# Two stacked transformer blocks on one core: the expert rows are scatter-added to the residual rows instead of being kept in slots and gathered at the end

## The chip, the core and the metric

One core of one Trainium2 chip runs the whole program. The metric is the device time of one execution in microseconds (us); lower is better. The engines are named as in the profile: PE (TensorE; PEld is its weight load), DVE (VectorE), ACT (ScalarE), POOL (GpSimd) and SP (SyncE, which issues most DMAs).

## The reference, cut to what matters

1024 tokens of width 1024 go through a first block of two layers and a second block with a gated mixer and a mixture of experts. The change touches the experts and the final norm:

```python
def _hier_moe(h, ...):            # h: 1024 tokens x 1024
    # softmax over 4 groups, the best group; softmax over its 8 experts, the best TOP_K = 2
    weights = g_p * e_p            # one weight for each (token, choice)
    # the 2048 (token, choice) pairs are sorted by expert and padded to blocks of 128
    yb = (silu(xb @ w_gate[e]) * (xb @ w_up[e])) @ w_down[e]   # hidden width 512
    y = zeros.at[tok_buf].add(yb * w_buf)
# around it:
x = x + gate2 * y
out = x * rsqrt(mean(x * x) + 1e-6) * final_norm_g
```

Counted from the reference on its own inputs, the 2048 pairs spread over the 32 experts with 26 to 129 pairs each (17 experts have 64 or more, one has more than 128).

## The kernel before, in words

The program is a row of stages with a barrier of all engines between them (`Env.run`). The last three matter here.

`stage_mix` writes the residual rows (`x3_rows`, a DRAM tensor of 1024 x 1024) and the normed rows (`n3_rows`). On the side SP stores zeros into a part of `y_slots`, six DMAs of 1280 KB (L2550).

`stage_experts` first routes (DVE, with a few small matmuls on PE): each of the 2048 pairs gets a slot, that is a block of 128 rows and a place in it. Block b < 32 belongs to expert b and is filled from its first partition on; block 32 takes what the fullest expert has over 128. There are `LOOPED` = 33 blocks; code for more stands behind an `If` that is not taken with these inputs. For each block b:

- POOL gathers 128 normed rows by index into `xg` (L3109);
- PE transposes them (L3002), ACT modulates and splits them in a high and a low part (L3167, L3146), DVE makes the low part (L3303);
- PE multiplies with the gate and the up weights, three matmuls (high-high, low-high, high-low) for each of 8 chunks, 24 each (L3007 to L3009);
- ACT applies silu (L3174), DVE multiplies by the up product (`hid`, L3353), PE transposes (L3023), ACT and DVE split again (L3185, L3307), and PE multiplies with the down weights, 24 more matmuls. The down product of block b-1 is made in step b, behind the up product of block b;
- DVE multiplies the result by `gate` into `yb` (`results`, L3314), and SP stores 512 KB of it to block b-1 of `y_slots` (L2926, for the last block L2946).

The weights come in six pieces of 1 MB for each expert: g0, g1, u0, u1, d0, d1. SP loads each to a landing tile as soon as DVE has set it free (L2900), ACT casts it to the high part (`hi`, L3142) when PE has done with the former contents, and DVE subtracts for the low part (`lo`, L3216). PE, ACT and SP run blocks 4 to 29 in a hardware loop; so does DVE. The order of the work on each engine is the order in which the code is written:

```python
def step(b, s):                      # DVE, before
    lo_x(b + 1); lo("g0", b + 1); lo("g1", b + 1)
    # waits for up_full, act_set
    hid = act_ * up_b
    lo("u0", b + 1); results(b - 1); lo("u1", b + 1)
    lo("d0", b); lo("d1", b); lo_h(b)
```

During the last block SP loads the eight tiles of residual rows (`cx`, L2910) and the final gain ahead (L2913).

`stage_combine` gathers, for each of 8 tiles of 128 tokens, the two weighted expert rows of each token from `y_slots` into `cy` (16 indirect DMAs of 512 KB on POOL, L3409). DVE adds the left half with two weighted adds (L3460, L3462), PE the right half in PSUM with diagonal matrices (L3418 to L3428), ACT takes the sums of squares (L3439, L3441) and the root (L3445), DVE scales (L3467, L3468), and SP stores (L3402).

## Time and profile before

| what | value |
|---|---|
| median of 3 runs | 2980.92 us (2980.89 to 2983.64) |
| the profiled execution: its own time | 2982.22 us |
| the profiled execution: its span | 2980.5 us |
| mean granted TensorE clock | 0.984 |
| busy share: PE, PEld, DVE, ACT, POOL | 95%, 72%, 58%, 42%, 15% |
| HBM read, written | 389.78 MB, 61.94 MB |
| experts: first matmul of block 0 to the end of the last | 2327.5 to 2932.3 us |
| last stage: first POOL gather to the end of the span | 2939.55 to 2980.5 us |

The page gives the shares of the whole span. What a change in one stage is worth is read from that stage alone: which wait ends last there, and what follows on it. "<-" in a row with brackets names what ended the idle time just before it.

### The profile page before, as it was taken

The numbers are of one execution on the slowest core, as the hardware profiler recorded it, in microseconds if no ns is written. First come the engines' busy times: TensorE is split into PE (matmuls) and PEld (weight loads), VectorE is DVE, ScalarE is ACT, GpSimd is POOL, SyncE is SP. The second block draws the span as 40 slices with busy tenths as digits, with TensorE's granted clock in tenths as the row PEclk, the third lists the DMA queues.
The fourth block names the chain that finished last, engine by engine and source line by source line (L and its number), as shares of the span: only waits on it lengthen the run. The fifth ranks groups of instructions, "written<-read, shape, count | busy, mean of one in ns | idle before, by whom it ended". The sixth has DMA issues, their size and how long they took to land. (4 is left out here: it accounts for less than half of the span.)

```text
span 2980.5 us, 47752 instructions
## 1 busy us (share of the span) xinstructions
PE 2825.3 (95%) x19536; PEld 2142.6 (72%) x19536; DVE 1739.4 (58%) x2511; ACT 1249.6 (42%) x2032; POOL 456.7 (15%) x354
## 2 busy tenths in 40 slices
PE   8999999999899999998999989999799899999996
PEld 6877744587677777776765566668678788888884
DVE  2332223386366666666435354353885899999995
ACT  2111100022355555554223122132443688888883
POOL 2222100031222222222230110101000100000002
PEclk9999999999999999999999999999899999999999
DMA  5111031474221221213131111103664799999997
GB/s 173 46 40 39 22 134 43 145 238 142 57 57 57 57 58 57 57 43 121 57 84 36 27 60 30 60 29 134 211 220 157 291 411 408 414 408 410 411 370 282
DMA packets 234173, 454.46 MB, mean 152 GB/s; under 512 B 18128, under 2 KB 159952, under 8 KB 208640
## 3 DMA queue, kind: packets, MB, share of 16 engines
q1 hardware_dynamic: 226928, 426.07, 39.9%
q0 software_dynamic: 7056, 25.69, 2.3%
q8 instruction: 140, 2.29, 0.3%
q14 instruction: 49, 0.40, 0.0%
HBM read 389.78 MB, written 61.94 MB: 152 GB/s over the span
## 5 line engine op out<-in xcount | busy, mean ns | idle before, releaser
L1020 PE MATMUL psum<-x_hi,w_hi 128*128 128x512 f32 x512 | 211.9, 414 | 10.1 <-POOL w_lo L1132 7.7
L1218 DVE TENSOR_TENSOR fox_pT_lo<-psum,fox_pT_hi 128x512 fp32r<-128x512 f32 (+2 forms) x192 | 107.1, 558 | 192.0 <-ACT fox_pT_hi L1157 182.7
L1022 PE MATMUL psum<-x_hi,w_lo 128*128 128x512 f32 x512 | 201.6, 394 | 0.0
L1021 PE MATMUL psum<-x_lo,w_hi 128*128 128x512 f32 x512 | 200.8, 392 | 0.0
L724 PE MATMUL psum<-wo,yT 128*128 128x512 f32 x384 | 167.9, 593 | 2.8 <-PEq L100 1.5
L1714 PE MATMUL psum<-hT,wr 128*128 128x512 f32 x384 | 167.1, 594 | 0.0
L3216 DVE TENSOR_TENSOR lo_g<-land_g,hi_g 128x2048 fp32r<-128x2048 f32 x66 | 148.3, 2288 | 18.5 <-ACT hi_g L3142 18.5
L3216 DVE TENSOR_TENSOR lo_u<-land_u,hi_u 128x2048 fp32r<-128x2048 f32 x66 | 150.6, 2285 | 0.0
L1168 ACT ACTIVATE fox_p<-fox_p,fox_bias 128x256 f32<-128x256 f32 (+7 forms) x128 | 99.6, 778 | 117.8 <-DVE fox_bias L1204 114.5
L3216 DVE TENSOR_TENSOR lo_d<-land_d,hi_d 128x2048 fp32r<-128x2048 f32 x66 | 148.3, 2289 | 0.7 <-ACT hi_d L3142 0.7
L179 PE MATMUL psum<-x_hi,w_hi 128*128 128x512 f32 x352 | 138.4, 393 | 0.0
L180 PE MATMUL psum<-x_lo,w_hi 128*128 128x512 f32 x352 | 137.9, 392 | 0.0
L724 PEld LDWEIGHTS psum<-wo,yT 128*128 128x128 f32 x384 | 72.3, 190 | 91.0 <-issue 88.7
L181 PE MATMUL psum<-x_hi,w_lo 128*128 128x512 f32 x352 | 137.6, 391 | 0.0
L1714 PEld LDWEIGHTS psum<-hT,wr 128*128 128x128 f32 x384 | 72.5, 190 | 88.1 <-issue 87.6
L3142 ACT CAST hi_d<-land_d 128x2048 fp32r<-128x2048 f32 x66 | 122.5, 1903 | 16.5 <-PE psum L3009 16.3
L1157 ACT CAST fox_pT_hi<-psum 128x512 fp32r<-128x512 f32 (+2 forms) x192 | 86.1, 484 | 102.4 <-PE psum L1048 102.3
L829 DVE SCALAR_TENSOR_TENSOR x_tile<-x_tile,psum 128x512 f32<-128x512 f32 x32 | 22.0, 688 | 180.8 <-PE psum L724 120.2
L3142 ACT CAST hi_g<-land_g 128x2048 fp32r<-128x2048 f32 x66 | 122.6, 1904 | 1.4 <-DMA land_g<-in_moe_w_gate 1.4
L3142 ACT CAST hi_u<-land_u 128x2048 fp32r<-128x2048 f32 x66 | 122.4, 1902 | 1.8 <-DMA land_u<-in_moe_w_up 1.8
L1763 PE MATMUL psum<-w_uv,hT 128*128 128x256 f32 x512 | 119.8, 388 | 0.2 <-issue 0.2
L2018 POOL TENSOR_TENSOR L<-abT,m_level 128x512 f32<-128x512 f32 x40 | 56.5, 1449 | 407.8 <-ACT abT L2108 407.8
(543 smaller groups left out, 7122.9 us busy)
## 6 DMA issues: line engine op xcount, KB each, us to landing
land_g<-in_moe_w_gate SPq DMA_DIRECT2D x66, 1024.0 KB, 7.8
land_u<-in_moe_w_up SPq DMA_DIRECT2D x66, 1024.0 KB, 7.3
land_d<-in_moe_w_down SPq DMA_DIRECT2D x66, 1024.0 KB, 9.0
ada<-in_ada_w SPq DMA_DIRECT2D x24, 1024.0 KB
y_slots<-yb SPq DMA_DIRECT2D x33, 512.0 KB, 9.9
w<-in_w_in SPq DMA_DIRECT2D x27, 512.0 KB, 4.1
w_land<-in_w_kv_shared SPq DMA_DIRECT2D x23, 512.0 KB, 4.2
w_land<-in_w_in SPq DMA_DIRECT2D x23, 512.0 KB, 3.8
```

The costliest lines, as they stand in the source:

```text
L179: self.nc.tensor.matmul(bank[:], hi[:, d, :], E.x_hi[:, d, cols], start=(d == 0), stop=False)
L180: self.nc.tensor.matmul(bank[:], hi[:, d, :], E.x_lo[:, d, cols], start=False, stop=False)
L181: last = self.nc.tensor.matmul(bank[:], lo[:, d, :], E.x_hi[:, d, cols], start=False, stop=(d == ND - 1))
L724: last = nc.tensor.matmul(banks[hf][:], E.yT[:, c, t * P:(t + 1) * P], rows, start=first, stop=final)
L1020: nc.tensor.matmul(bank[:], hi[:, d, :], E.x_hi[:, d, cols], start=(d == 0), stop=False)
L1021: nc.tensor.matmul(bank[:], hi[:, d, :], E.x_lo[:, d, cols], start=False, stop=False)
L1022: last = nc.tensor.matmul(bank[:], lo[:, d, :], E.x_hi[:, d, cols], start=False, stop=(d == ND - 1))
L1218: V.tensor_tensor(pT_lo[j][:, s0:s1, half], ringT.bank(("t", n, j, s0))[:, 0:(s1 - s0) * P].rearrange("p (s n) -> p s n", n=P), pT_hi[j][: ...
L1714: last = nc.tensor.matmul(bank[:], w[m % NW][:, d, :], E.hT[:, d, hf * HALF:(hf + 1) * HALF], start=(d == 0), stop=(d == ND - 1))
L1763: last = nc.tensor.matmul(bank[:, 0:UVW], E.hT[:, d, t * P:(t + 1) * P], w_uv[:, d, :], start=(d == 0), stop=(d == ND - 1))
L3142: nc.scalar.copy(w_hi[x][:], land[x][:]).then_inc(hi_set[x], 1)
L3216: V.tensor_tensor(w_lo[x][:], land[x][:], w_hi[x][:].bitcast(F32), ALU.subtract).then_inc(lo_set[x], 1)
```

## The change

- The expert rows go no longer to `y_slots`. DVE multiplies each row of a block by its own weight too (`of_slot`, one scalar per partition and block; `results` is now a scalar_tensor_tensor), and POOL adds the block to `x3_rows` by an indirect DMA with an add (`add_block`). Places of a block without a pair have a row index past the bound and are not written. Each add waits for the one before. On POOL, the add of block b-4 stands behind the gather of block b.
- The weights of the slots come from 32 small matmuls (`weights_of_slots`), which PE does in step 0 between the up product and the transposes of `hid`. Their operands lie in the not yet used d0 tiles.
- In DVE's step 0, `hid` stands before `lo` of g0 and g1. DVE's loop over the blocks is written out.
- The last block's down weights are split into the g0 and g1 tiles (`kept_in`), so ACT need not wait for the down product of block 31; DVE's `results` of block 31 stands behind these splits. Before the last down product PE has six small matmuls more.
- The zeros in `stage_mix`, the loads of `cx` ahead, and the gathers, adds and matmuls of `stage_combine` are gone: SP now loads the eight tiles in that stage, ACT squares whole rows, DVE scales them, SP stores.

```diff
-                        part = slice((t - 2) * ZEROS, (t - 1) * ZEROS)
-                        sp.dma_start(further[:, part, :], zeros[:]...).then_inc(zeroed, 16)
...
+        def kept_in(x, b):
+            return "g" + x[1] if x[0] == "d" and isinstance(b, int) and b == LOOPED - 1 else x
...
-                    if not (isinstance(b, int) and b == 0):
-                        sp.wait_ge(M["y_set"], b)
-                        sp.dma_start(y_of(b - 1), yb[1 - s][:]).then_inc(y_out[1 - s], 16)
                     if isinstance(b, int) and b + 1 == LOOPED:
-                        sp.wait_ge(M["up_full"], LOOPED - 1)
-                        for t in range(NT - 2):
-                            rows_ahead(t)
...
+                        for x in UP_PIECES:
+                            sp.wait_ge(lo_set[x], LOOPED)
                         gain_ahead()
...
+                def weights_of_slots():
+                    pe.wait_ge(R["at_weight"], TOP_K)
+                    for n in range(TOP_K * NT):
+                        k, t = n // NT, n % NT
+                        for i in range(2):
+                            last = nc.tensor.matmul(rank_b[:, 0:TABLE], at_part[k][:, t, :], at_weight[k][i][:, t, :],
+                                                    start=(n == 0 and i == 0), stop=(n == TOP_K * NT - 1 and i == 1))
+                    last.then_inc(R["of_slot"], 1)
...
+                for _ in range(6):
+                    nc.tensor.matmul(gate_b[:, 0:P], E.ident[:], E.ident[:], start=True, stop=True)
                 down_of(LOOPED - 1)
...
+                add = lambda b, y: nc.gpsimd.indirect_dma_start(x_rows[:, :], bass.IndirectOffsetOnAxis(ap=row[:, b:b + 1], axis=0), y[:], None,
+                                                                bounds_check=S - 1, oob_is_err=False, compute_op=ALU.add)
+                def add_block(b):
+                    pool.wait_ge(M["y_set"], b + 1)
+                    if b >= 1:
+                        pool.wait_ge(y_out[(b - 1) % 2], 16 * ((b - 1) // 2 + 1))
+                    add(b, yb[b % 2]).then_inc(y_out[b % 2], 16)
...
+                    if b >= 4:
+                        add_block(b - 4)
+                for b in range(LOOPED - 4, LOOPED):
+                    add_block(b)
...
+                    if kept_in(x, b) != x:
+                        act.wait_ge(M["gate_full"], LOOPED)
...
-                    V.tensor_tensor(yb[s][:], down_rows, gate[:], ALU.mult).then_inc(m["y_set"], 1)
+                    V.scalar_tensor_tensor(yb[s][:], down_rows, of_slot[:, of_block], gate[:], ALU.mult, ALU.mult).then_inc(m["y_set"], 1)
...
             @block.sync
+                for t in range(NT):
+                    sp.dma_start(x[t][:], rows[t * P:(t + 1) * P, :]).then_inc(E.cx_landed[t], 16)
...
             @block.scalar
+                    act.wait_ge(E.cx_landed[t], 16)
+                    nc.scalar.activation(sq[:], x[t][:], ACT.Square, accum_out=ss[:, b]).then_inc(ss_set, 1)
                     act.wait_ge(ss_set, t + 1)
+                    nc.scalar.activation(dev[:, b], ss[:, b], ACT.Sqrt, bias=E.eps_rms[:], scale=1.0 / D).then_inc(dev_set, 1)
...
             @block.vector
+                    dve.wait_ge(dev_set, t + 1)
+                    link(dve, V.reciprocal(inv[:, b], dev[:, b]))
+                    V.scalar_tensor_tensor(x[t][:], x[t][:], inv[:, b], gain[:], ALU.mult, ALU.mult).then_inc(ready, 1)
```

How the order of the instructions moves, at three places.

ACT, the end of block 31 and block 32 (`hi_d` and `hi_g` are the high tiles of the down and gate weights, `land_d` the landing tile), before:

```order
L3174 ACTIVATE e_act<-psum 128x512
L3142 CAST hi_d<-land_d 128x2048 x2
L3185 CAST e_h_hi<-psum 128x512
L2871 TENSOR_LOAD n_over
L2871 ISA x2
```

and with the change:

```order
L3178 ACTIVATE e_act<-psum 128x512
L3146 CAST hi_g<-land_d 128x2048 x2
L3189 CAST e_h_hi<-psum 128x512
L2864 TENSOR_LOAD n_over
L2864 ISA x2
```

The casts keep their place; their target is another tile, and with it the wait is for the gate product of block 32 in place of the down product of block 31.

DVE, around step 0 (`e_act` holds `hid`, `e_x_lo` the low part of the next block's tokens, `weight` the pairs' weights), before:

```order
L3339 TENSOR_TENSOR den<-den,gprob 128x8
L3340 TENSOR_TENSOR weight<-den,top 128x8
L3341 TENSOR_TENSOR weight<-den,top 128x8
L3303 TENSOR_TENSOR e_x_lo<-e_xm,e_x_hi 128x1024
L3216 TENSOR_TENSOR lo_g<-land_g,hi_g 128x2048 x2
L3353 TENSOR_TENSOR e_act<-e_act,psum 128x512
L3216 TENSOR_TENSOR lo_u<-land_u,hi_u 128x2048 x2
L3216 TENSOR_TENSOR lo_d<-land_d,hi_d 128x2048 x2
L3307 TENSOR_TENSOR e_h_lo<-psum,e_h_hi 128x512
```

and with the change (the rows L3351 to L3356, which stand twice, set the operands of the small matmuls in the d0 tile):

```order
L3351 CAST weight_hi<-weight 128x8
L3352 TENSOR_TENSOR weight_lo<-weight,weight_hi 128x8
L3354 TENSOR_TENSOR lo_d<-iota_j,block_f 128x384
L3355 TENSOR_TENSOR lo_d<-lo_d,weight_lo 128x384
L3356 TENSOR_TENSOR lo_d<-lo_d,weight_hi 128x384
L3323 TENSOR_TENSOR e_x_lo<-e_xm,e_x_hi 128x1024
L3380 TENSOR_TENSOR e_act<-e_act,psum 128x512
L3220 TENSOR_TENSOR lo_g<-land_g,hi_g 128x2048 x2
L3220 TENSOR_TENSOR lo_u<-land_u,hi_u 128x2048 x2
L3220 TENSOR_TENSOR lo_d<-land_d,hi_d 128x2048 x2
L3327 TENSOR_TENSOR e_h_lo<-psum,e_h_hi 128x512
```

`e_act` now stands ahead of the two `lo_g`. Ahead of `e_x_lo` two groups of five rows replace thirteen small ones: of these, the eight on `weight` now stand behind the first `lo_g` of block 0, and the five on `ovexp` (with the copy of `of_slot`) behind `e_h_lo`.

POOL, the last gathers of the experts and what follows (`cy` are the gathered expert rows of the last stage), before:

```order
L3109 DMA xg<-n_rows,idx 128x1024 x33
L3115 TENSOR_LOAD n_over
L3115 ISA x2
L3116 COMPARE_AND_BRANCH
L3109 DMA xg<-n_rows,idx 128x1024 x14
L3116 UNCONDITIONAL_BRANCH
L99 ISA
L3405 UNCONDITIONAL_BRANCH
L3409 DMA cy_0<-y_slots,slot 128x1024 x2
L3409 DMA cy_1<-y_slots,slot 128x1024 x2
```

and with the change:

```order
L3092 DMA xg<-n_rows,idx 128x1024
L3093 DMA x_rows<-yb,row 1024x1024
L3092 DMA xg<-n_rows,idx 128x1024
L3093 DMA x_rows<-yb,row 1024x1024 x5
L3112 TENSOR_LOAD n_over
L3112 ISA x2
L3113 COMPARE_AND_BRANCH
```

From the fifth block on, each gather is followed by an add; after the last gather five adds stand alone, and the sixteen gathers of the last stage are gone.

## Rows read from the trace of the kernel before

**Rows 1.** The chain of waits, its longest piece; columns: start, length, what.
```profile
2960.39 11.65 DMA cy<-y_slots,slot
```
**Rows 2.** Stretches: length, busy time by engine, PE clock, DMA share, GB/s.
```profile
2650.00:2667.87 17.87, 17.87 (x86) 14.97 (x86) 16.86 (x11) 15.86 (x18) 0.97 (x1) 1.00 1.01 398
2667.87:2685.73 17.86, 17.86 (x85) 14.74 (x84) 16.86 (x11) 15.85 (x18) 0.97 (x1) 1.00 1.01 422
```
**Rows 3.** The same view, stretches of 4 us inside one block.
```profile
2663.00:2667.00 4.00, 4.00 (x19) 3.30 (x19) 4.00 (x2) 4.00 (x3) 0.00 (x0) 1.00 1.00 347
...
2671.00:2675.00 4.00, 4.00 (x21) 3.32 (x21) 4.00 (x3) 2.20 (x3) 0.00 (x0) 1.00 1.02 429
```
**Rows 4.** All waits from 2370 to 2900 us: total, times, longest.
```profile
ACT e_act L3174 <- PE psum L3009: 53.6, 30, 1.9
DVE e_x_lo L3303 <- ACT e_x_hi L3146: 12.9, 30, 0.5
```
**Rows 5.** Time from issue to landing of `land_d`, 2640 to 2680 us.
```profile
DMA to landing us min/median/max: 8.9/9.4/10.1
```
**Rows 6.** The page's DMA queues: packets, MB, share of 16 engines' span.
```profile
q1 hardware_dynamic: 226928, 426.07, 39.9%
q0 software_dynamic: 7056, 25.69, 2.3%
```
**Rows 7.** PE in order of time, start of the experts: start, length.
```profile
2315.42 1.88 PE L2995 MATMUL psum<-at_block,e_x_hi 128*128 128x48 f32 x8
...
2344.76 1.08 PE L3023 MATMUL psum<-ident,e_act 128*128 128x128 f32 x4 [5.15 <-DVE e_act L3353]
```
**Rows 8.** DVE in order of time, start of the experts.
```profile
2324.74 1.37 DVE L3318 TENSOR_SCALAR e_xm<-psum,mod_rows 128x128 f32<-128x128 f32 x4 [2.79 <-PE psum L3002]
...
2357.18 1.23 DVE L3303 TENSOR_TENSOR e_x_lo<-e_xm,e_x_hi 128x1024 fp32r<-128x1024 f32 x1 [3.06 <-ACT e_x_hi L3146]
```
**Rows 9.** The last block in order of time, by engine.
```profile
2908.09 2.55 SPq L2900 DMA_DIRECT2D land_d<-in_moe_w_down  x2
...
2917.66 3.70 ACT L3142 CAST hi_d<-land_d 128x2048 fp32r<-128x2048 f32 x2 [10.29 <-PE psum L3009]
...
2919.59 4.49 DVE L3216 TENSOR_TENSOR lo_d<-land_d,hi_d 128x2048 fp32r<-128x2048 f32 x2 [0.71 <-ACT hi_d L3142]
...
2924.01 0.69 DVE L3307 TENSOR_TENSOR e_h_lo<-psum,e_h_hi 128x512 fp32r<-128x512 f32 x1
...
2924.75 0.80 PE L3007 MATMUL psum<-hi_d,e_h_hi 128*128 128x512 f32 x1 [6.64 <-DVE e_h_lo L3307]
...
2932.35 1.23 DVE L3314 TENSOR_TENSOR yb<-psum,gate 128x1024 f32<-128x1024 f32 x1 [7.66 <-PE psum L3009]
...
2933.61 0.34 SPq L2946 DMA_DIRECT2D y_slots<-yb  x1
```
**Rows 10.** Landing of d1 of block 32, issued at 2910.3 us.
```profile
DMA to landing us min/median/max: 8.4/8.4/8.4
```
**Rows 11.** Landing of the last `y_slots` store, issued at 2933.6 us.
```profile
DMA to landing us min/median/max: 3.4/3.4/3.4
```
**Rows 12.** Stretches behind PE's idle times: columns as in rows 2.
```profile
2345.00:2348.00 3.00, 3.00 (x10) 2.52 (x10) 3.00 (x2) 3.00 (x2) 0.00 (x0) 0.50 1.03 385
2924.80:2928.30 3.50, 3.50 (x8) 2.77 (x9) 0.00 (x0) 0.00 (x0) 0.00 (x0) 0.50 1.03 414
```
**Rows 13.** Landing of the first `cy` gather, issued at 2939.55 us.
```profile
DMA to landing us min/median/max: 4.8/4.8/4.8
```
**Rows 14.** The last stage in order of time, ACT and DVE.
```profile
2949.44 1.28 ACT L3445 ACT_TABLE_LOAD   x1
...
2954.16 0.63 ACT L3439 ACTIVATE c_sq<-cx 128x512 f32<-128x512 f32 x1 [1.29 <-issue]
...
2976.13 0.75 DVE L3468 SCALAR_TENSOR_TENSOR cx<-psum,c_inv,final_gain 128x512 f32<-128x512 f32 x1
```
**Rows 15.** The last stage, a stretch with gathers and stores together; columns as in rows 2.
```profile
2960.00:2964.00 4.00, 3.04 (x7) 0.97 (x6) 3.04 (x7) 1.90 (x7) 1.42 (x2) 1.00 1.02 416
```

More of the change, by code:

```diff
@@ L2804, in stage_experts @@
         token_id = sb("token_id", [P, NT])
-        part_i, part, block_i, block_f = sb("part_i", [P, NT], I32), sb("part", [P, NT]), sb("block_i", [P, NT], I32), sb("block_f", [P, NT])
+        slot, part_i, block_i = (sb(x, [P, NT], I32) for x in ("slot", "part_i", "block_i"))
+        part, block_f = sb("part", [P, NT]), [sb(f"block_f{k}", [P, NT]) for k in range(TOP_K)]
+        weight = [sb(f"weight{k}", [P, NT]) for k in range(TOP_K)]
+        weight_hi, weight_lo = ([sb(f"weight_{x}{k}", [P, NT], F32R) for k in range(TOP_K)] for x in ("hi", "lo"))
+        unfilled, of_slot = sb("unfilled", [P, BLOCKS]), sb("of_slot", [P, BLOCKS])
         TABLE = BLOCKS + BLOCKS % 2
@@ L2824, in stage_experts @@
         passed = yb[1][:, EXPERTS * NT:EXPERTS * (NT + S // P - 1)].rearrange("p (e j) -> p e j", j=S // P - 1)
[L2826 removed]
+        R = {x: E.sem("route_" + x) for x in ("consts", "gsub", "gexp", "ssub", "sexp", "both", "ranks", "places", "table", "idx", "over", "masks", "at_weight", "of_slot", "xm0", "xh0", "xl0", "xm1")}
         two = lambda name: [E.sem(f"{name}{i}") for i in range(2)]
@@ L2953, in begin @@
                         sp.wait_ge(lo_set[x], LOOPED)
-                    for t in range(NT - 2, NT):
-                        sp.wait_ge(E.cx_landed[t], 16)
                     sp.wait_ge(E.gain_landed, 16)
@@ L3024, in turn_h, with down @@
                     last.then_inc(full, 1)
-                def down(full, ready):
+                def down(full, ready, kept=lambda x: x):
                     for n, x in enumerate(DOWN_PIECES):
                         ready(x)
+                        of_hi, of_lo = (chunks(w[kept(x)][:], x) for w in (w_hi, w_lo))
                         for h in range(2):
@@ L3032, in down @@
                                 c = n * NHC // 2 + k
-                                last = three(down_b[h][:], h_hi[:, c, :], h_lo[:, c, :], chunks(w_hi[x][:], x)[:, k, cols], chunks(w_lo[x][:], x)[:, k, cols],
+                                last = three(down_b[h][:], h_hi[:, c, :], h_lo[:, c, :], of_hi[:, k, cols], of_lo[:, k, cols],
                                              c == 0, c == NHC - 1)
@@ L3059, in step @@
                     into_hidden(up_b, "u1", s, ready, 1, True).then_inc(M["up_full"], 1)
-                    if not (isinstance(b, int) and b == 0):
+                    if isinstance(b, int) and b == 0:
+                        weights_of_slots()
+                    else:
                         down_of(b - 1)
@@ L3345, in step @@
                     more = not (isinstance(b, int) and b + 1 >= LOOPED)
+                    first = b == 0
                     if more:
                         lo_x(M, b + 1, 1 - s)
+                    if more and not first:
                         lo("g0", b + 1)
@@ L3353, in step @@
                     V.tensor_tensor(hid[:], act_[:], up_b[:], ALU.mult).then_inc(M["hid_set"], 1)
+                    if first:
+                        lo("g0", b + 1)
+                        lo("g1", b + 1)
                     if more:
                         lo("u0", b + 1)
-                    if not (isinstance(b, int) and b == 0):
-                        results(M, b - 1, 1 - s)
                     if more:
+                        if not (isinstance(b, int) and b == 0):
+                            results(M, b - 1, 1 - s)
                         lo("u1", b + 1)
@@ L3361, in step @@
                     lo("d1", b)
+                    if not more:
+                        results(M, b - 1, 1 - s)
                     lo_h(M, b)
-                blocks_in_turn(dve, step)
+                    if isinstance(b, int) and b == 0:
+                        dve.wait_ge(R["of_slot"], 1)
+                        link(dve, V.tensor_copy(of_slot[:], rank_b[:, 0:BLOCKS]))
+                        blocks_over()
+                for b in range(LOOPED):
+                    step(b, b % 2)
                 filled = blocks_filled(dve)
@@ L3378, in further, with stage_combine @@
                     results(O, j, 0)
-                further_blocks(dve, filled, lambda: dve.wait_ge(y_out[0], 16 * (EXPERTS // 2 + 1)), further)
+                with dve.If(filled > 1):
+                    dve.wait_ge(y_out[0], 16 * (EXPERTS // 2 + 1))
+                    for j in range(OVER - 1):
+                        further(j)
                 E.chain_n = link.n
-def stage_combine(nc, E, A, y_slots):
+def stage_combine(nc, E, A, rows):
     with ExitStack() as st:
```

178 lines of the change are left out of this document (59 added, 119 removed).

## The prediction

> **What bounds the kernel now.** I read the chain of waits first. Its longest piece is one wait of 11.65 us for the last gathered expert rows [rows 1]: the last stage is set by DMA. In it 16 gathers of 0.5 MB and 8 stores of 0.5 MB move 12.6 MB between 2939.55 and 2980.5 us, and where both kinds run together the rate is 416 GB/s [rows 15].
>
> The stretches of the experts show the other 600 us: two blocks of 17.87 us each in which PE is busy all the time, at full clock, with 398 and 422 GB/s of DMA beside it [rows 2]. PE is the bound there, but DMA is close behind. Inside a block it reaches 429 GB/s and falls to 347 in one stretch [rows 3]; the mean of rows 2 is 410, so some 3 to 4% of a block, 0.6 to 0.7 us, is left on the DMA engines. The reader is to see this number as the one that decides: the change takes a plain store out of each block and puts a read-modify-write in.
>
> The waits say how the other engines stand: ACT waits 1.8 us per block for PE (53.6 us in 30 waits), DVE 0.43 us for ACT (12.9 in 30), and nobody waits for a landing [rows 4], though a down piece needs 9.4 us to land [rows 5].
>
> **The change part by part.** The sum is made against the profiled execution (2982.22 us, span 2980.5). The median of the runs is 2980.92, 1.3 below it; I apply the difference to the median.
>
> *Zeros in the mix stage.* Six DMAs of 1280 KB go. No engine waits for them; PE and DVE work beside them. 0; if a stream load behind them gains, at most about 1 us.
>
> *Start of the experts.* DVE gets two small instructions and the eight on the weights ahead of `e_xm`, some 2.1 us, where it idled 2.79 us for the gathered tokens [rows 8]: 0. Ahead of `e_x_lo` of block 1 it has ten rows instead of thirteen, about 0.6 us longer, for which an idle gap of 0.46 us stood there. The five on `ovexp` fall in the idle 3.06 us ahead of the next `e_x_lo` [rows 8]: 0. PE idled 5.15 us for `hid` [rows 7]; `hid` now comes about 4.5 us earlier, and PE does 32 matmuls of 48 columns in its place, each 1.88 / 8 = 0.235 us at most [rows 7], so up to 7.5 us, and 6.8 by the spacing. That is 1.6 to 2.3 us later; but PE no longer idles, and the gate product behind the gap ran 3 us at a granted 0.50, the 1.2 GHz level [rows 12], which cost about 1.5 us. Together +0.5 us, range -1 to +2.
>
> *Each block, PE's and DVE's side.* `results` becomes a scalar_tensor_tensor. The 512-wide one took 0.75 us [rows 14], so 1024 wide it takes 1.3 to 1.5 us instead of 1.23 [rows 9]. The excess of 0.1 to 0.3 us hides in DVE's 0.43 us wait [rows 4]: 0. If that cover were gone it would be at most 0.3 x 31 = 9 us.
>
> *Each block, DMA's side.* A 4 KB row costs 0.023 x 16 x 2980.5 / 6272 = 0.175 us of an engine (49 indirect DMAs of 128 rows are 6272 [rows 6]); the plain queue gives 0.18 us per 4 KB. The store of 128 rows is 8 rows per engine, 1.4 us of each. The adds carry only the 2048 filled rows, 64 per block; if a row that is read and written costs two row times, that is 128 row times, as before. So the bounds: below, one row time each and evenly spread, 0.7 us per engine less, which gains nothing because PE is the bound; above, see the rivals. I take 0. The queue side is free: POOL issues one gather of 0.97 us per block [rows 2]; an add may need the 10 us that a transfer takes here to land, and the next waits for it only 17.87 us later.
>
> *Last block.* PE stood 6.64 us for DVE's `h_lo` of block 32, behind ACT's casts, which waited 10.29 us for the down product of block 31 [rows 9]. That wait goes. Next late is the data: d0 and d1 are issued at 2908.1 and 2910.3 [rows 9], and d1 landed 8.4 us later, at 2918.7 [rows 10]. Without the 512 KB store issued beside it I take 7.2 us: 2917.5. Then cast 1.9, `lo` 2.3, `h_lo` 0.7 [rows 9] and `results` of block 31, 1.3: PE resumes at 2923.7 instead of 2924.75, -1.0 us. Of the idle time 5 us remain, and both idle stretches of 5.15 and 6.64 us were followed by 3 to 4 us at 0.50 [rows 7, 9, 12], so I let the six small matmuls gain nothing; if the clock stays up, the first 9 matmuls gain 1.8 us (8 in 3.5 us there, 19 in 4 us at full clock [rows 3]). Range of the term -3.5 to 0.
>
> *Last add in place of the last store.* `yb` is ready near 2932.7. The store needed 3.4 us to land [rows 11], a gather of 128 rows 4.8 [rows 13]. This add writes one row (one expert has 129 pairs), but reads it first: between them, 4.4 us, so 2937.1, against 2937.0 before. So +1.0 us against a start moved by -1.0, range -1 to +2. The Trainium skill's page "DMA: Bandwidth & Descriptors", section on the anatomy of one DMA, gives about 2.0 us plus bytes over 436 GB/s for a DMA of this path; by it, behind 1 us of issue, the sum would be 1.4 us lower. The gather of rows 13, 1.0 + 2.0 + 1.2 = 4.2 by that rule, took 4.8.
>
> *Last stage.* The first gather of the old stage was issued at 2939.55, 2.5 us behind the last landing, POOL's own start included; SP has only the barrier, so I set its first load at 2938.7. First tile lands 4.8 us later at worst, 2943.5. ACT per tile: the 512-wide square took 0.63 us [rows 14], so 1024 wide up to 1.26, and 1.1 if part of the 0.63 is fixed; with the read of the sum and the root 1.5. Eight tiles and one table load of 1.28 [rows 14] end at 2956.8; DVE adds 0.2 + 1.4 and the last store 3.6 (2976.9 to 2980.5): 2962.0. DMA moves 8.4 MB instead of 12.6: at 416 GB/s [rows 15] 20.2 us, behind 2.3 us of start and 1 of landing, 2962.2. I take 2962.5. So -18.0 us. Bounds: at 330 GB/s, the mean of the old stage, 2967; with neither rate in the way, 2960.
>
> Sum: 0 + 0.5 + 0 + 0 - 1.0 + 1.0 - 18.0 = -17.5. Predicted median 2980.9 - 17.5 = **2963.4 us**. Own range of this case 2957 to 2970.
>
> **The rivals.** A difference under 0.2%, 6 us, is no change here.
>
> *A: the adds crowd some DMA engines.* A block's rows fill from partition 0, and the experts have 64 pairs in the mean. If the engine follows the partition, nearly all rows fall to half the engines, 7 to 8 each; at two row times 2.6 us instead of 1.4, less the free 0.65: 0.4 to 0.6 us more per block, for 31 blocks 12 to 18 us. That gives 2975 to 2982. If the unfilled rows are moved too, it is 8 rows on every engine, the same 0.75 us, 2986. For it speaks that DMA stands at 1.01 [rows 2]; against, that it needs both the doubling and the crowding. The Trainium skill's page "DMA: Bandwidth & Descriptors", section "The descriptor swizzle", has the engine follow the partition in this way, with partitions 0 to 63 on engines 0 to 7, for plain transfers; no row here shows an engine.
>
> *B: the add is slow per row.* If a read-modify-write is not pipelined and costs over two row times, DMA becomes the bound and casts wait for landings in every block. At three row times, 7.5 rows x 0.53 = 4.0 us: 4.0 - 1.4 - 0.65 = 1.9 us per block, 60 us, which gives 3023. It turns the sum positive from 17.5 / 31 = 0.56 us per block on. For it: the trace has no such DMA at all. Against: gathers by index cost what plain rows cost [rows 6].
>
> *C: the last stage starts late or runs slowly.* The last two adds wait for one another and for `results` of block 31, now behind the down splits; each 2 us more, and the loads at the 330 GB/s of before: 2968 to 2971.
>
> *D: the clock stays up and d1 lands early:* 2957 to 2960.
>
> **How the numbers follow.** The forecast's case 0.51, C 0.08, D 0.05, A 0.17, B 0.19. A lies half below 2975 (faster) and half above. Faster: 0.51 + 0.08 + 0.05 + 0.08 = 0.72; within 0.2% (2975 to 2987) 0.08; slower 0.20. The range reaches from D to the end of A, 2957 to 2986, and leaves out B.
>
> **What would show it.** Blocks still 17.87 us apart with PE never idle; no wait of ACT for `land_d` before block 32; the casts of block 32's down weights right behind their landings; PE idle 5 us ahead of the last down product; the last stage some 24 us long, the eight loads first. The forecast is wrong if a block grows by over 0.1 us, if ACT waits for landings in each block, or if an add needs more than 17 us to land.

## The result, and the profile after

The changed kernel takes 2990.8 us (median of 10 runs, 2988.7 to 2996.2), beside 2980.9 us of the kernel before (10 runs): ratio 1.0033, 95% interval 1.0024 to 1.0042. It is slower by 9.9 us, where 2963.4 was forecast. The profiled execution took 2994.22 us, its span is 2992.4, 11.9 longer than the 2980.5 before.

The stages ahead of the experts are the same code but for the zeros, and POOL's first gather of the experts came between 2313.9 and 2322.9 us in the profiled executions of this case, so the parts are measured from that gather, a point of the kernel itself:

| from, to | before | after | difference | forecast |
|---|---|---|---|---|
| first gather to the end of the last `yb` | 2317.83 to 2933.58: 615.75 | 2318.02 to 2954.99: 636.97 | +21.2 | -0.4 |
| last `yb` to the first DMA of the last stage | to 2939.55: 5.97 | to 2967.63: 12.64 | +6.7 | 0.0 |
| that to the end of the span | to 2980.5: 40.95 | to 2992.4: 24.77 | -16.2 | -17.2 |

(The forecast's start and last block stand in the first row; the second is 2932.7 to 2938.7, 6.0 us, by the `yb` that it assumed; the third is 2938.7 to 2962.5.) The last stage is what was forecast, to 1 us. The blocks are not.

Stretches of 100 us of the blocks, columns as in [rows 2], first before, then after:

```profile
2500.00:2600.00 100.00, 100.00 (x470) 83.17 (x470) 94.01 (x57) 89.77 (x92) 4.86 (x5) 1.00 1.01 411
```

```profile
2400.00:2500.00 100.00, 99.26 (x465) 81.65 (x464) 93.22 (x55) 85.94 (x94) 23.45 (x12) 1.00 1.01 389
2500.00:2600.00 100.00, 97.08 (x448) 79.36 (x448) 88.69 (x54) 85.47 (x94) 19.89 (x10) 1.00 0.99 375
2600.00:2700.00 100.00, 96.52 (x446) 78.55 (x445) 90.76 (x54) 84.33 (x88) 19.79 (x10) 1.00 1.00 381
```

PE had no idle time before and now has 1 to 3%. The DMA share is 1.0 in both, but the rate fell by 7%, from 412 to 382 GB/s in the mean of 2400 to 2800 us. The waits of the changed kernel from 2376 to 2900 us, which answer to [rows 4]:

```profile
ACT hi_d L3146 <- DMA land_d<-in_moe_w_down: 41.4, 54, 1.7
DVE e_x_lo L3323 <- ACT e_x_hi L3150: 31.0, 29, 1.6
ACT hi_u L3146 <- DMA land_u<-in_moe_w_up: 28.1, 23, 1.7
PE psum L2992 <- DVE e_act L3380: 11.8, 21, 1.0
```

ACT's wait for PE, 51.8 us in this window before, fell to 3.0; ACT waits for landings instead, DVE then for ACT, PE for DVE. The DMA view from 2400 to 2800 us, before and then after (queues: packets, MB, share of 16 engines; issues: size, median time to landing):

```profile
q1 hardware_dynamic: 22671, 153.11, 93.3%
q0 software_dynamic: 3168, 11.54, 7.8%
...
land_u<-in_moe_w_up SPq DMA_DIRECT2D x46, 1024.0 KB, 7.1
land_d<-in_moe_w_down SPq DMA_DIRECT2D x44, 1024.0 KB, 9.0
```

```profile
q1 hardware_dynamic: 18646, 135.76, 85.7%
q0 software_dynamic: 6070, 16.85, 14.3%
...
land_u<-in_moe_w_up SPq DMA_DIRECT2D x44, 1024.0 KB, 12.3
land_d<-in_moe_w_down SPq DMA_DIRECT2D x43, 1024.0 KB, 13.3
x_rows<-yb,row POOLq DMA_INDIRECT x22, 11.7
```

Fewer bytes move, and a down piece lands 4.3 us later, an up piece 5.2. The 22 adds moved 5.3 MB, some 1300 rows, for 6.5% of 16 engines in 400 us: 416 us, 0.32 us a row. That is the two row times that the forecast assumed, and only the filled rows move. So the price of a row was right, the number too. What was left open is which engines carry them.

The tail, in order of time:

```profile
2953.71 1.28 DVE L3337 SCALAR_TENSOR_TENSOR yb<-psum,of_slot,gate 128x1024 f32<-128x1024 f32 x1 [8.68 <-PE psum L2978]
2955.76 1.55 POOL L3093 DMA_INDIRECT x_rows<-yb,row  x1 [9.00 <-DVE yb L3337]
2967.63 4.53 SPq L3438 DMA_DIRECT2D cx<-x_rows  x8
2971.16 1.06 ACT L3449 ACTIVATE c_sq<-cx 128x1024 f32<-128x1024 f32 x1 [29.76 <-DMA cx<-x_rows]
```

The landing of that add, counted from its issue:

```profile
DMA to landing us min/median/max: 4.2/4.2/4.2
```

So it landed at 2960.0, and the last stage's first load came 7.7 us later. POOL waits for that landing, reads the count of filled blocks and passes the untaken `If` (1.0 us, to 2961.0). Then comes its `DRAIN`, the instruction with which each engine ends a stage ahead of the barrier. It took 5.45 us, and the barrier opened right behind it, at 2966.5; clearing the semaphores and the second barrier took the last 1.2 us. The same row of the kernel after, and of the kernel before (its line there is L2882; columns: count, ns min/median/max, first and last start):

```profile
L2875 POOLq DRAIN  x1: 5450/5450/5450, 2961.0 to 2961.0; - x1
```

```profile
L2882 POOLq DRAIN  x1: 10111/10111/10111, 2855.1 to 2855.1; - x1
```

Before the change POOL had no work behind its last gather, so its `DRAIN` of 10.1 us was over at 2865.2, some 72 us ahead of the barrier. Now it stands on the path. Why it takes POOL so long is not shown.

### The profile page after: what moved, and what is told of

It is laid out like the page before. It is cut to its first block and busy times, and to the rows that moved or that the text cites. A ratio compares the mean times of both kernels' runs of the same rounds, so it can differ in the third digit from the quotient of the medians.

```text
span 2992.4 us, 47562 instructions
## 1 busy us (share of the span) xinstructions
PE 2816.2 (94%) x19532; PEld 2141.5 (72%) x19532; DVE 1729.6 (58%) x2492; ACT 1246.5 (42%) x2000; POOL 539.1 (18%) x370
## 5 line engine op out<-in xcount | busy, mean ns | idle before, releaser
L1020 PE MATMUL psum<-x_hi,w_hi 128*128 128x512 f32 x512 | 211.7, 413 | 11.3 <-POOL w_lo L1132 9.0
L3093 POOL DMA_INDIRECT x_rows<-yb,row x33 | 96.1, 2911 | 462.7 <-DVE yb L3337 462.7
## 6 DMA issues: line engine op xcount, KB each, us to landing
land_g<-in_moe_w_gate SPq DMA_DIRECT2D x66, 1024.0 KB, 10.1
land_d<-in_moe_w_down SPq DMA_DIRECT2D x66, 1024.0 KB, 13.3
wo<-in_w_out SPq DMA_DIRECT2D x11, 1024.0 KB, 10.5
```

The source lines that it names most:

```text
L1020: nc.tensor.matmul(bank[:], hi[:, d, :], E.x_hi[:, d, cols], start=(d == 0), stop=False)
```

## The experiments

Theory 1: the rows of an add fall to half of the DMA engines, which then carry 8 rows x 0.32 us = 2.6 us per block instead of 1.3, and the weights wait for these engines. The rivals: POOL's issue (2.85 us each, the queue, the descriptors) disturbs the loads (theory 2); or the amount of read-modify-write does, wherever it runs (theory 3).

| kernel | median us | ratio to before, 95% interval | first gather to last `yb` | to first DMA of last stage | rest |
|---|---|---|---|---|---|
| e1 first spread | 2986.6 | 1.0023 (1.0011 to 1.0034) | 628.9 | 12.9 | 24.6 |
| e2 no rows | 2971.6 | 0.9967 (0.9955 to 0.9979) | 614.6 | 13.2 | 24.5 |
| e3 plain scatter | 2971.3 | 0.9963 (0.9949 to 0.9978) | 613.5 | 11.4 | 24.4 |
| e4 128 rows in each add | 2996.3 | 1.0055 (1.0042 to 1.0069) | 635.1 | 15.5 | 24.9 |
| e5 interleaved | 2972.3 | 0.9969 (0.9959 to 0.9979) | 614.5 | 12.8 | 25.1 |
| e6 POOL's end reordered | 2989.1 | 1.0029 (1.0018 to 1.0040) | 635.1 | 12.0 | 24.7 |
| e7 e5 and e6 | 2972.1 | 0.9975 (0.9966 to 0.9984) | 617.1 | 12.2 | 24.6 |
| e8 e7, `kept_in` undone | 2973.6 | 0.9980 (0.9970 to 0.9990) | 616.2 | 12.2 | 24.7 |
| e9 e7, last add gone | 2969.9 | 0.9960 (0.9948 to 0.9973) | 614.6 | 6.9 | 25.4 |
| e10 e7, SP waits | 2972.9 | 0.9967 (0.9954 to 0.9979) | 616.1 | 9.0 | 24.5 |
| e11 e10, loads ahead | 2964.2 | 0.9949 (0.9936 to 0.9962) | 616.4 | 5.0 | 23.6 |
| e13 e11, three ahead | 2967.3 | 0.9953 (0.9938 to 0.9969) | 615.0 | 3.9 | 25.7 |

The intervals reach 3 to 5 us to either side; where an edit moves less, its segment of the one profiled execution is read, and such a reading has no interval. Part of the column "first gather to last `yb`" is the last block, which varies for reasons of its own. Up to the start of `results` of block 30 the blocks took 584.6 us before, 605.2 in the changed kernel, 603.7 in e6 (the same blocks), 598.4 in e1, 604.5 in e4, 584.1 and 584.0 in e2 and e3, and 583.9 to 585.9 in e5 and the six kernels built on it. (e12, the same kernel as e13, left no result.)

**e1, places spread in a first way.**

```diff
-                    V.tensor_scalar(part_i[:], slot[:], P - 1, None, ALU.bitwise_and)
+                    link(dve, V.tensor_scalar(part_i[:], slot[:], 15, 3, ALU.bitwise_and, ALU.logical_shift_left))
+                    link(dve, V.tensor_scalar(part_hi[:], slot[:], P - 1, 4, ALU.bitwise_and, ALU.logical_shift_right))
+                    link(dve, V.tensor_tensor(part_i[:], part_i[:], part_hi[:], ALU.bitwise_or))
```

> The changed kernel with one thing else: the place of a slot in its block is spread over the partitions (place r goes to partition (r % 16) * 8 + r // 16), so a block with 64 rows fills partitions in all sixteen groups of eight instead of the first 64. Theory 1 (crowding): the adds slow the blocks because their rows, 0.33 us each, fall to half of the 16 DMA engines, and the weight loads wait for the slowest engine. Spread, an engine has 4 rows instead of 8, 1.3 us instead of 2.6; a block falls from about 18.5 back to 17.9 us, and the time from 2990.8 by 31 x 0.6 = 19 to 2970 to 2974. ACT's waits for land_d and land_u nearly go. Theory 2 (POOL: the issue of 2.85 us and its descriptors disturb the loads, whatever the rows do): no change, 2990 to 2992. Theory 3 (a read-modify-write slows all traffic by its amount, wherever it runs): no change, 2990 to 2992.

It was 2986.6: 4 us of the 19. The isolated add of block 31 shows why. Nothing else uses the DMA engines then (columns as in [rows 2]); first the changed kernel, then e1:

```profile
2947.00:2948.00 1.00, 1.00 (x4) 0.81 (x3) 0.00 (x0) 0.00 (x0) 0.00 (x0) 0.50 0.64 41
2948.00:2949.00 1.00, 1.00 (x4) 0.81 (x3) 0.00 (x0) 0.00 (x0) 0.00 (x0) 0.50 0.43 61
2949.00:2950.00 1.00, 1.00 (x4) 0.71 (x4) 0.00 (x0) 0.00 (x0) 0.00 (x0) 0.50 0.54 106
2950.00:2951.00 1.00, 1.00 (x4) 0.81 (x3) 0.00 (x0) 0.00 (x0) 0.00 (x0) 0.50 0.34 66
```

```profile
2942.00:2943.00 1.00, 1.00 (x4) 0.82 (x4) 0.00 (x0) 0.00 (x0) 0.00 (x0) 0.75 0.45 70
2943.00:2944.00 1.00, 1.00 (x6) 0.78 (x6) 0.00 (x0) 0.00 (x0) 0.00 (x0) 1.00 0.50 98
```

Only about half of the 16 engines are busy in both, for the same 67 rows (0.27 MB): this spread did not spread. So the run does not test theory 1 as it was meant to. That the blocks still took 7 us less (598.4 against 605.2) may come from the blocks with fewer than 64 rows, which this spread deals evenly to its eight engines; that was not tried apart.

**e2 and e3, the rows taken out, and the rows without the add.**

```diff
-                link(dve, V.tensor_scalar(unfilled[:], rank_b[:, 0:BLOCKS], 0.0, float(4 * S), ALU.is_equal, ALU.mult))
+                link(dve, V.tensor_scalar(unfilled[:], rank_b[:, 0:BLOCKS], 0.0, float(4 * S), ALU.is_ge, ALU.mult))
```

```diff
-                                                                bounds_check=S - 1, oob_is_err=False, compute_op=ALU.add)
+                                                                bounds_check=S - 1, oob_is_err=False)
```

> The changed kernel with every row index past the bound: all 33 adds are issued, but none moves a row (left out of the computation: the experts' part of the result). Theory 1 (crowding) and theory 3 (amount of read-modify-write): blocks back to 17.9 us or a little less, 2969 to 2973, issues on POOL still 2.85 us each. Theory 2 (POOL's issue and the descriptors): no change, 2989 to 2992, with the landings of the weights as late as now.

> The changed kernel with the same indirect DMAs but without their add: rows are written over the residual rows (left out of the computation: the sum). A row should then take 0.16 us of an engine instead of 0.33. Theory 1 (crowding): 8 rows x 0.16 = 1.3 us on the busiest engine, as the old store had; blocks 17.9 us, 2970 to 2974. Theory 2 (POOL's issue): no change, 2990 to 2992. Theory 3: as theory 1, 2970 to 2974.

2971.6 and 2971.3. POOL's issues are still there (2.85 us each in e2, 2.28 in e3), the loads are not disturbed: theory 2 falls. A block stretch of e2, and ACT's wait from 2376 to 2900 us, are those of the kernel before:

```profile
2500.00:2600.00 100.00, 100.00 (x470) 83.08 (x469) 94.10 (x58) 89.64 (x93) 19.43 (x10) 1.00 0.99 380
```

```profile
ACT e_act L3178 <- PE psum L2978: 51.8, 29, 1.9
```

In e3 the queue's share is 11.3% for 17.81 MB, 3.5% more than the gathers alone for 6.27 MB: 224 us for 1531 rows, 0.15 us each, half of a row that is added. Theories 1 and 3 both stand.

**e4, 128 rows in each add.**

```diff
-                                                                bounds_check=S - 1, oob_is_err=False, compute_op=ALU.add)
+                                                                bounds_check=S + P - 1, oob_is_err=False, compute_op=ALU.add)
...
+                link(dve, V.tensor_scalar(far[:], token_id[:, 0:1], float(S), None, ALU.add))
-                link(dve, V.tensor_scalar(unfilled[:], rank_b[:, 0:BLOCKS], 0.0, float(4 * S), ALU.is_equal, ALU.mult))
+                link(dve, V.tensor_scalar(unfilled[:], rank_b[:, 0:BLOCKS], 0.0, far[:], ALU.is_equal, ALU.mult))
...
-        x3_rows = nc.dram_tensor("x3_rows", (S, D), F32, kind="Internal").ap()
+        x3_rows = nc.dram_tensor("x3_rows", (S + P, D), F32, kind="Internal").ap()
```

> The changed kernel with 128 rows in every add: a place without a pair adds its zeros to rows of its own behind the 1024 residual rows (a longer DRAM tensor), so twice the rows are read and written. Theory 1 (crowding): the busiest engine had 8 rows already and has 8 now, only the others catch up; hardly any change, 2990 to 2996. Theory 3 (amount): twice the disturbance, 31 x 0.6 us more, 3009 or above. Theory 2 (POOL's issue): no change, 2990 to 2992.

2996.3, at the edge of theory 1's range; first gather to last `yb` took 635.1 us, no longer than the 637.0 of the changed kernel, with twice the rows. Theory 3 asked for about 656 there (637.0 + 31 x 0.6). The rest of the 5 us is in the tail, where the last add now moves 128 rows, and in the spread of the medians. In its isolated add nearly all 16 engines are busy, and the rate is about twice that of the changed kernel's:

```profile
2943.00:2944.00 1.00, 1.00 (x4) 0.81 (x3) 0.00 (x0) 0.00 (x0) 0.00 (x0) 0.61 0.90 127
2944.00:2945.00 1.00, 1.00 (x6) 0.79 (x5) 0.00 (x0) 0.00 (x0) 0.00 (x0) 1.00 0.98 197
```

**e5, places interleaved by the bits that select the engine.**

```diff
-                    V.tensor_scalar(part_i[:], slot[:], P - 1, None, ALU.bitwise_and)
+                    V.tensor_scalar(part_i[:], slot[:], 1, 6, ALU.bitwise_and, ALU.logical_shift_left)
+                    V.tensor_scalar(bits[0][:], slot[:], 14, 1, ALU.bitwise_and, ALU.logical_shift_left)
+                    V.tensor_scalar(bits[1][:], slot[:], 48, 4, ALU.bitwise_and, ALU.logical_shift_right)
+                    link(dve, V.tensor_scalar(bits[2][:], slot[:], 64, 1, ALU.bitwise_and, ALU.logical_shift_right))
+                    V.tensor_tensor(part_i[:], part_i[:], bits[0][:], ALU.bitwise_or)
+                    link(dve, V.tensor_tensor(bits[1][:], bits[1][:], bits[2][:], ALU.bitwise_or))
...
+                    link(dve, V.tensor_tensor(part_i[:], part_i[:], bits[1][:], ALU.bitwise_or))
```

> The changed kernel with the places of a slot dealt to partitions in another way: place r goes to the partition whose bits 6, 2, 3, 4 are the low four bits of r, bits 0, 1, 5 the next three. The isolated adds of the first spread still had 8 to 9 rows in flight, as the changed kernel, and the adds of 128 rows had 17; that fits an engine that goes by bits 6 and 4 to 2 of the partition, of which the first spread left bit 2 at zero. (The Trainium skill's page on DMA, section on the descriptor swizzle, states this for a plain transfer.) Theory 1 (crowding, by these bits): now 4 to 5 rows per engine and about 16 in flight at the end; a block falls to 17.9 us, the wait for land_d and land_u nearly goes; 2971 to 2975. Theory 3 (amount of read-modify-write): as the first spread, 2985 to 2988. Theory 4 (an indirect DMA with skipped rows uses half the engines whatever the place): 8 to 9 in flight, 2985 to 2991.

2972.3, 18.5 us less than the changed kernel, and now faster than the kernel before by 0.31% (interval 0.21 to 0.41). The isolated add and a block stretch, and the waits from 2376 to 2900 us:

```profile
2922.00:2923.00 1.00, 1.00 (x4) 0.71 (x3) 0.00 (x0) 0.00 (x0) 0.00 (x0) 0.50 0.81 66
2923.00:2924.00 1.00, 1.00 (x6) 0.83 (x5) 0.00 (x0) 0.00 (x0) 0.00 (x0) 0.95 0.92 147
...
2500.00:2600.00 100.00, 100.00 (x474) 83.30 (x473) 95.13 (x57) 88.40 (x93) 22.32 (x11) 1.00 1.01 400
```

```profile
ACT e_act L3178 <- PE psum L2978: 41.0, 29, 1.9
ACT hi_d L3146 <- DMA land_d<-in_moe_w_down: 9.4, 17, 1.1
```

The same rows, as many, by the same adds; only the partitions differ (the gathers move 128 rows either way). Theory 1 is shown, theories 3 and 4 fall. ACT's wait for a down piece did not vanish, but PE is never idle. Bit 6 of the partition helps to choose the engine, since rows in the first 64 partitions kept to half of them; so does bit 2, which the first spread left at zero; bit 5 does not, since it is zero for the first 64 rows here and all 16 engines work. That the other two are bits 4 and 3, and not 1 and 0, no run here tells apart. Bits 6 and 4 to 2 are the rule in the Trainium skill's page "DMA: Bandwidth & Descriptors", section "The descriptor swizzle", given there for a plain transfer; as far as they go, these runs agree for an indirect add with skipped rows.

**e6, e7 and e8, POOL's end, both, and the last block's casts.**

```diff
-                for b in range(LOOPED - 4, LOOPED):
-                    add_block(b)
-                pool.wait_ge(y_out[0], 16 * (EXPERTS // 2 + 1))
                 pool.wait_ge(R["over"], 1)
                 filled = pool.value_load(n_over[0:1, 0:1], min_val=0, max_val=OVER)
+                for b in range(LOOPED - 4, LOOPED):
+                    add_block(b)
                 with pool.If(filled > 1):
...
+                pool.wait_ge(y_out[0], 16 * (EXPERTS // 2 + 1))
```

```diff
         def kept_in(x, b):
-            return "g" + x[1] if x[0] == "d" and isinstance(b, int) and b == LOOPED - 1 else x
+            return x
```

> The changed kernel with POOL's end of the experts in another order: the count of filled blocks is read ahead of the last four adds, and the untaken If stands ahead of the wait for the last add's landing instead of behind it. Theory 1 (POOL's own instructions, the read and the If, fill most of the 6.1 us between that landing and the first load of the last stage): they now run while the add lands; the last stage starts 3 to 5 us earlier, 2986 to 2988. Theory 2 (the 6.1 us are the barrier and the landing's own signal): no change, 2990 to 2992.

> Both edits: places interleaved, and POOL's end reordered. If each does what its first theory says: 2991 - 18 - 4 = 2969, range 2966 to 2972, faster than the kernel before. If neither does: 2985 to 2991.

> Both edits, and the last block's down weights again in the d0 and d1 tiles (kept_in gives x itself), so ACT's casts wait for the down product of block 31. Theory 1 (the term of the prediction, -1.0 us for the early casts, by their landing): 1 us slower than with both edits alone, up to 3 where the landings come early. Theory 2: the casts wait for the landings anyway: no change.

e6: the segment behind `yb` went from 12.6 to 12.0 us, not to 8 to 9: POOL's read and `If` are not what fills it. Its `DRAIN` still took 5.45 us behind the landing. The median, 2989.1, lies between the two theories' ranges. e7 gave nothing over e5 and came out just above its range, 2972.1 where 2966 to 2972 was expected; its last down product ran longer. From `h_lo` to `yb` the same 24 matmuls took 7.2 us in e5 and 8.7 in e7, behind 4.42 and 4.24 us of idle time. They began at 2920.22 and 2923.53, and PE's clock came back after 2.9 us in the one and 6.2 in the other (columns: length, PE busy, PE clock, DMA share, GB/s; e5, then e7):

```profile
2922.16:2923.16 1.00, 1.00 (x4) 0.53 1.03 90
2923.16:2924.16 1.00, 1.00 (x5) 1.00 0.79 143
```

```profile
2928.48:2929.48 1.00, 1.00 (x4) 0.50 0.00 0
2929.48:2930.48 1.00, 1.00 (x5) 0.88 0.00 0
```

e8: from the start of `results` of block 30 to the last down product it took 23.5 us (2903.78 to 2927.30), with `kept_in` 21.3 (2902.26 to 2923.53), before the change 22.3 (2902.44 to 2924.75). But the other kernels with `kept_in` and spread places took 21.3 to 22.2 (e5, e9, e10, e11, e13). So the early casts are worth 0.1 to 1.0 us against the old order, and 1.3 to 2.3 against their own undoing; the median of e8 is 1.5 higher, which its interval does not tell from nothing. In the changed kernel itself it was 21.9, within that spread.

**e9, e10, e11 and e13, what the last add costs, and who waits for it.**

```diff
-                for b in range(LOOPED - 4, LOOPED):
+                for b in range(LOOPED - 4, LOOPED - 1):
                     add_block(b)
+                pool.wait_ge(M["y_set"], LOOPED)
+                pool.wait_ge(y_out[1], 16 * (EXPERTS // 2))
...
```

```diff
                 further_blocks(sp, filled, begin, further, end)
+                sp.wait_ge(y_out[0], 16 * (EXPERTS // 2 + 1))
...
-                pool.wait_ge(y_out[0], 16 * (EXPERTS // 2 + 1))
```

```diff
                 sp.wait_ge(y_out[0], 16 * (EXPERTS // 2 + 1))
+                for t in range(NT):
+                    sp.dma_start(E.cx[t][:], x_rows[t * P:(t + 1) * P, :]).then_inc(E.cx_landed[t], 16)
...
-                for t in range(NT):
-                    sp.dma_start(x[t][:], rows[t * P:(t + 1) * P, :]).then_inc(E.cx_landed[t], 16)
```

(The first of these is e9, the second e10, the third e11, which has the second too; e13 has `range(3)` there, the other five loads behind the barrier, and PE's 6 and 24 small matmuls are out.)

> The kernel with both edits, without the add of block 32 (left out of the computation: its one row). POOL still waits for that block's yb and for the add of block 31, long landed. It shows what the last add costs from yb to the start of the last stage. Theory 1 (the add is the price: issue 1.5, landing 4.2 behind it): yb to first load falls from 12.2 to 6.3 us, the time by 6, 2966. Theory 2 (the add's landing is hidden by something else that needs 10 us at the end of the stage): under 2 us, 2970 to 2972.

> The kernel with both edits, but SP waits for the last add's landing and POOL does not. Theory 1 (POOL wakes late or has work behind its wait): the first load of the last stage 2 to 5 us earlier, 2967 to 2970. Theory 2 (the 5.7 us between that landing and the first load are the stage's end for any engine: clearing of semaphores, barrier, code of the next stage): no change, 2972.

> As the one before, and SP issues the eight loads of residual rows right behind its wait, in the experts' stage, ahead of the barrier. If the end of the stage takes 5.7 us behind the landing, the loads now run beside it: first tile at hand when the last stage starts, 3.5 us of its landing and up to 2 us more gone, 2966 to 2969. If the time of the last stage is set by its own DVE work from the barrier on, the gain stays at 3.5 us. No gain only if the wait for the add itself is what takes the time.

> As the one before, but SP issues only three of the eight loads ahead of the barrier and five behind it, and PE's 6 small matmuls ahead of the last down product and its 24 behind it are gone. In the run before, ACT's first square started at 2949.69, 5.5 us behind the first load: SP came to the barrier only behind 4.1 us of issues. Theory 1 (SP's issues held the barrier): the barrier opens 2 us earlier and the first landing, 3.5 us, decides; yb to the end of the span 1.5 to 2 us shorter, 2961 to 2963. Theory 2 (the barrier takes its 4 us anyway): no change, 2964. The small matmuls are worth nothing by the granted clock of 0.50 behind every gap: the last down product should take 7.9 to 9.4 us with or without them.

e9: 5.3 us of the 12.2 go; the median fell by 2, short of the 6 of theory 1. Of the 6.9 that stay, 0.4 pass until POOL's `DRAIN` starts, 5.4 are that `DRAIN`, and 1.2 the rest of the stage's end. So POOL's `DRAIN` stands on the path even without the last add, since POOL waits for the last `yb`. PE's 24 small matmuls behind the last down product end 4.1 us behind `yb`, ahead of it. In the kernel before they are the row here, and then the first work of its last stage:

```profile
2932.16 5.52 PE L3089 MATMUL psum<-ident 128*128 128x128 f32 x48
2933.61 0.34 SPq L2946 DMA_DIRECT2D y_slots<-yb  x1
2938.86 0.30 PEld L3418 LDWEIGHTS psum<-cx,ident 128*128 128x128 f32 x2 [1.37 <-issue]
```

They ended at 2937.7, behind the last store's landing at 2937.0 [rows 11]: before the change these matmuls were the later of the two, and the last store was hidden. The add stands on the path with its issue and its landing, and POOL's `DRAIN` behind it. Row of e9, then of e10:

```profile
L2875 POOLq DRAIN  x1: 5371/5371/5371, 2937.9 to 2937.9; - x1
```

```profile
L2875 POOLq DRAIN  x1: 7110/7110/7110, 2931.6 to 2931.6; - x1
```

e10: the segment fell from 12.2 to 9.0 us. A wait of POOL for its own add, ahead of the barrier, cost 3.2 us more here than a wait of SP for the same landing; the medians do not tell the two apart. The trace shows why: with SP waiting, POOL's `DRAIN` starts with the issue of the add and runs beside its landing. It took 7.1 us, to 2938.7, the landing came at 2936.0, and the first load at 2939.9, 1.2 us behind the `DRAIN`. So the 4 us between landing and load are mostly this `DRAIN`; behind the last engine that comes to it, the end of the stage took 1.1 to 1.2 us. e11 issues the loads ahead of the barrier, rows in order of time:

```profile
2937.90 1.28 DVE L3347 SCALAR_TENSOR_TENSOR yb<-psum,of_slot,gate 128x1024 f32<-128x1024 f32 x1 [8.55 <-PE psum L2982]
2939.94 1.55 POOL L3097 DMA_INDIRECT x_rows<-yb,row  x1 [8.87 <-DVE yb L3347]
2944.20 4.13 SPq L2946 DMA_DIRECT2D cx<-x_rows  x8
2949.69 1.06 ACT L3457 ACTIVATE c_sq<-cx 128x1024 f32<-128x1024 f32 x1 [23.97 <-PEq L100]
```

ACT waits for the barrier (L100). POOL's `DRAIN` ended at 2947.0, and SP came behind eight issues at 2948.4, so here SP is the last, by 1.4 us. From the last `yb` to the end of the span it takes 28.6 us instead of 36.8 in e7, and 2964.2 is 16.4 us under the 2980.6 of the kernel before on that chip (0.51%, interval 0.38 to 0.64), under its expected 2966 to 2969 and the lowest median of all, though its interval and that of e13 overlap. e13's barrier did open earlier, ACT's first square came 9.0 us behind `yb` instead of 10.5. Only now POOL is the last again: its `DRAIN` ended at 2944.3, SP was there at 2941.7.

```profile
L2875 POOLq DRAIN  x1: 7062/7062/7062, 2937.3 to 2937.3; - x1
```

The end did not follow: 29.6 us behind `yb`, and 2967.3 lies above both theories. DVE began its last tile 21.8 us behind `yb` instead of 23.3, but the stores landed 6.2 us behind their issue instead of 3.7, at the rate of DMA:

```profile
2954.00:2958.00 4.00, 0.00 (x0) 0.00 (x0) 3.89 (x7) 3.75 (x9) 0.00 (x0) 0.50 1.01 414
2958.00:2962.00 4.00, 0.00 (x0) 0.00 (x0) 1.59 (x3) 0.00 (x0) 0.00 (x0) 0.50 1.02 419
```

The 8.4 MB at 415 GB/s take 20.2 us, so DMA sets the end here. The pause between the first three loads and the other five fits the loss: the DMA share was 0.79 from 2946 to 2950 us, against 1.01 in e11. That it is the cause was not tried apart. `h_lo` to `yb` took 8.3 us without the small matmuls and 7.2 to 8.7 in the kernels with them.

## Why the prediction was wrong

By its own steps:

- **Zeros, start of the experts, PE's and DVE's side of a block:** forecast +0.5. With no rows moved (e2), first gather to the start of `results` of block 30 is 584.1 us against 584.6: -0.5. Right, within 1 us.
- **Each block, DMA's side: "I take 0".** This step failed. It priced a row rightly (two row times, measured 0.32 us against 0.15) and counted the rows rightly, but then set 128 row times against 128 as a mean over 16 engines. The rows fall mostly to eight. On those it is 8 x 0.32 = 2.6 us a block instead of 1.3, against a free margin of 0.6 to 0.7: an estimate of +0.65 a block. (Counted by its packets, each block's add has 26 to 128 rows; by bits 6 and 4 to 2 the first 36 rows already give the busiest engine its eight. 16 blocks have 64 or more, one fewer than was counted ahead.) Measured up to block 30: 605.2 - 584.6 = +20.6 us over 31 blocks, 0.66 each; in e6, the same blocks, 19.1; with the places spread it is -0.7 to +1.3 in all. The medians say 18.5 us between the changed kernel and e5. Rival A had this mechanism and nearly this price, 0.4 to 0.6 us, and got a chance of 0.17 because it "needs both the doubling and the crowding". The doubling was assumed in the main sum already, and that blocks fill from partition 0 with a mean of 64 rows stands in the kernel. What no row of before showed is that the engine follows the partition. That was the one open risk, and it was priced as two.
- **Last block, -1.0:** -0.4 in the changed kernel, and -0.1 to -1.0 where the adds are spread. From `h_lo` to `yb` it then took 8.7 us against 7.7: the clock stayed at 0.50 for 6 us, not 3 to 4 [rows 12], which is +1.0 that the sum does not have. The one kernel without the small matmuls (8.3 us) lies within the others' 7.2 to 8.7, so no gain of them shows.
- **Last add in place of the last store, +1.0:** this term was mis-sized. The landing, 4.2 us from the issue, was as forecast (4.4). But the issue began 0.8 us behind `yb`, and 7.7 us lie between the landing and the first load, where 1.6 were allowed: 1.0 for POOL's read and `If`, 5.45 for its `DRAIN`, 1.2 for the rest of the stage's end. The prediction has no term for the `DRAIN`, which lay hidden at 2855 us before. Before, the store's landing was hidden behind PE's small matmuls, and POOL's first gather came 1.9 us behind these. In all +6.7.
- **Last stage, -18.0:** -16.2 from its first DMA, against -17.2; the rest of the term was the earlier start. (The "330 GB/s, the mean of the old stage" of its upper bound is a misreading: 12.6 MB in 40.95 us are 307.)

Rival A's time, 2975 to 2982, left out the tail: with the 7 us of it, its upper end comes to 2989, against 2990.8. Half of A was counted as "faster", though its own times are all within 0.2% of the kernel before. Rival B falls, since a row costs about two row times; its price of 7.5 rows on an engine took the crowding of A for granted without saying so, and with rows spread over 16 engines it would have been near nothing. C had the right place, a late start, and about the size (5 to 8 us), but another cause. The sum with the measured terms, of the blocks, the last block, its down product, the tail and the last stage: 20.6 - 0.4 + 1.0 + 6.7 - 16.2 = +11.7, against 11.9 between the spans.

The observation named ahead as what would make the forecast wrong (ACT waiting for landings in each block, a block grown by over 0.1 us) is what the profile shows.

## What to carry to other kernels

Where a DMA moves only some partitions, count its time on the busiest engine, not as a mean over 16: rows in the first 64 partitions used half of them, and dealing the places out by bits 6 and 4 to 2 of the partition gave back all of it, for a few small integer operations. When a transfer at the end of a stage is exchanged for another one, ask first what hid the old one, and what its issuing engine still has to do behind it. Here it helped to let SP, which needs the data, wait for it, so that POOL's `DRAIN` ran beside the landing. If one risk in a list of rivals is already an assumption of the main sum, its chance is not a product of two.

## What the runs showed of the hardware

- Beside the weight loads an indirect DMA with an add took 0.32 us of an engine per row of 4 KB, without the add 0.15. Alone on the engines, the 67 rows of block 31's add took 31 us of an engine in all (27.9% of 16 engines in 7 us), 0.47 each. The last add landed 3.1 to 4.7 us behind its issue with its one row, and 4.8 with none (e2), so its landing is not the price of the row. The issue of an add takes POOL 2.85 us in the blocks and 1.55 at their end, the gather's 1.1 in the blocks. What makes the difference was not tried.
- Rows past the bound cost next to nothing on the DMA engines: with all skipped (e2) the adds' queue had a share of 7.9%, the 7.8% of the gathers alone.
- POOL's `DRAIN` at the end of the experts took 5.4 us behind its last wait, though the last add had landed or, in e9, been issued 8.8 us before, and 7.1 us when it started with the issue of the add. Why was not tried.
- The DMA share does not show slack. It is 1.01 at 411 GB/s before the change, 0.99 at 380 in e2, where nobody waits for a landing, and 0.99 at 375 in the changed kernel, where everybody does. The time to landing (9.0 against 13.3 us for a down piece) told them apart, the share did not. Why it stays at 1.0 while half the engines are the slower ones is open.
- After idle times of 4.2 to 4.4 us PE stayed at 0.50 for 2.9 us in one kernel and 6.2 in the other, with the same work behind it.
